# Retention in a 5-block transformer kernel: tokens on partitions for values and outputs

## The reference

```python
q, k, v, g = jnp.split(h @ w_in, [hk, 2 * hk, 2 * hk + hv], axis=-1)   # 4 heads: q, k 256 wide, v, g 512 wide
q = rotary(q); k = rotary(k) * (RET_KEY_DIM ** -0.5)                   # 256 ** -0.5 = 0.0625
o_fwd = retention_scan(q, k, v, log_gamma[0], True)                    # decay gamma ** (i - j), j <= i
o_bwd = flip(retention_scan(flip(q), flip(k), flip(v), log_gamma[1], False))
o = o_fwd + o_bwd
mu = jnp.mean(o, axis=-1, keepdims=True)
var = jnp.mean(jnp.square(o - mu), axis=-1, keepdims=True)             # per token and head, over 512 channels
o = ((o - mu) * lax.rsqrt(var + EPS)) * gn_g
return (jax.nn.silu(g) * o) @ w_out
```

## Time and profile before

| | |
|---|---|
| time, median of 3 runs | 3336.67 us (3329.39 to 3336.78) |
| profiled execution | 3337.88 us, of which the span of instructions 3335.9 us |
| PE busy | 3210.7 us, 96% |
| DVE, POOL, ACT busy | 1979.4, 1575.2, 1135.4 us |
| weight matmuls | 12096 (4032 tiles of three) |
| mean granted TensorE clock | 0.985 of full speed |

### The profile page before, as it was taken

One profiled execution on the slowest core, in us unless ns is written; L12 is line 12 of the kernel. 1 busy time (PEld: TensorE's weight loads), 2 busy tenths in 40 slices (PEclk: granted clock), 3 DMA queues, 4 the chain that ended last, 5 costly groups with the idle time before them and its releaser, 6 DMA issues. The chain is left out here.

```text
span 3335.9 us, 35062 instructions
## 1 busy us (share of the span) xinstructions
PE 3210.7 (96%) x13881; PEld 2471.9 (74%) x13881; DVE 1979.4 (59%) x2907; ACT 1135.4 (34%) x1686; POOL 1575.2 (47%) x764
## 2 busy tenths in 40 slices
PE   8889999998999999999999998898999999899999
PEld 5657888865778877777878776676778876587887
DVE  5464111288776584449477723423686588877756
ACT  5453222345422235543222322322322235542222
POOL 3224544566454453335554523433454556645454
PEclk9999999999999999999999999999999999999999
DMA  4212333321232333223332312222232332123232
GB/s 176 67 45 76 101 95 97 93 70 51 78 102 87 97 99 108 86 67 91 99 101 86 116 51 64 70 63 70 70 101 89 95 95 71 49 82 101 89 95 89
DMA packets 80675, 286.03 MB, mean 86 GB/s; under 512 B 9088, under 2 KB 9344, under 8 KB 80384
## 3 DMA queue, kind: packets, MB, share of 16 engines
q1 hardware_dynamic: 80512, 283.80, 27.2%
HBM read 281.40 MB, written 2.10 MB: 85 GB/s over the span
## 5 line engine op out<-in xcount | busy, mean ns | idle before, releaser
L2149 POOL TENSOR_TENSOR WL<-RAW,WH 128x1024 fp32r<-128x1024 f32 x504 | 1243.4, 2470 | 1362.1 <-ACT WH L1461 1361.6
L1243 PE MATMUL PS<-XH,WH 128*128 128x512 f32 x2768 | 1135.7, 410 | 44.2 <-POOL WL L2149 38.8
L1245 PE MATMUL PS<-XH,WL 128*128 128x512 f32 x2768 | 1088.0, 393 | 0.0
L1244 PE MATMUL PS<-XL,WH 128*128 128x512 f32 x2768 | 1087.8, 393 | 0.0
L1243 PEld LDWEIGHTS PS<-XH,WH 128*128 128x128 f32 x2768 | 525.5, 190 | 221.1 <-issue 89.7
L1461 ACT ACTIVATE WH<-RAW 128x1024 fp32r<-128x1024 f32 x504 | 526.5, 1049 | 430.6 <-PE PS L1245 430.0
L1244 PEld LDWEIGHTS PS<-XL,WH 128*128 128x128 f32 x2768 | 526.1, 190 | 114.6 <-issue 14.2
L1245 PEld LDWEIGHTS PS<-XH,WL 128*128 128x128 f32 x2768 | 525.0, 190 | 114.0
L1243 PE MATMUL PS<-HH,WH 128*128 128x512 f32 x1264 | 500.9, 396 | 15.4 <-DVE HL L2046 9.6
L1244 PE MATMUL PS<-HL,WH 128*128 128x512 f32 x1264 | 494.4, 391 | 0.0
L1245 PE MATMUL PS<-HH,WL 128*128 128x512 f32 x1264 | 494.3, 391 | 0.0
(11 more groups left out here) (225 smaller groups left out, 2359.3 us busy)
## 6 DMA issues: line engine op xcount, KB each, us to landing
RAW<-wst SPq DMA_DIRECT2D x504, 512.0 KB, 3.5
BI<-natb SPq DMA_DIRECT2D x16, 384.0 KB, 4.6
X<-xin SPq DMA_DIRECT2D x16, 256.0 KB, 5.0
X<-cmpw SPq DMA_DIRECT2D x1, 2048.0 KB, 9.5
out<-X SPq DMA_DIRECT2D x8, 256.0 KB, 2.1
BI<-relm SPq DMA_DIRECT2D x4, 448.0 KB, 10.0
PRM<-prm SPq DMA_DIRECT2D x1, 685.0 KB, 12.4
BI<-rope SPq DMA_DIRECT2D x2, 256.0 KB, 4.0
```

The lines of the kernel that those rows point to most:

```text
L1243: e.matmul(o, wh, h, start=first, stop=False)
L1244: e.matmul(o, wh, l, start=False, stop=False)
L1245: t = e.matmul(o, wl, h, start=False, stop=last)
L2149: e.tensor_tensor(WL[:, b % NSPLIT, :], RAW[:, b % NRAW, :], WH[:, b % NSPLIT, :].bitcast(f32), SUB).then_inc(*did(lo_made, ("lo", b)))
```

## The change

What it does, all inside the retention layer and the layout of its weights:

- Weights of v are laid out so that a block holds one input chunk's 512 output columns of the head. `by_tokens` takes four tiles at once and issues `mac_tokens` four times, once per group of 128 tokens, into four banks: the tokens' slice is stationary, the 512 weight columns move. ACT evacuates each bank with the per-token factor as a per-partition scale (`to_values`). `to_tokens` is gone from this layer.
- `rs_tokens` turns the per-token factor once by four transposes to get it on partitions (G8 columns 4 to 7). `rope_scale` multiplies cos and sin by the factor once, and `rotate_1` and `rotate_2` multiply straight from the PSUM bank, so q and k need no `scaled`. The factor 0.0625 moves into the product of `ret_scores`.
- The scores are deferred steps due 8, 11, 14 and 17 tiles into the value tiles, the values come as deferred beats among the gates' tiles (6, 10, 14, 18, 22).
- `ret_values` has PT stationary and the values moving: the bank holds 128 tokens by 512 channels. `bn_stats` and `bn_aggr` read mean and variance from it along the free axis, ACT makes the reciprocal root of one column, and `ret_centre` evacuates with both as per-partition scalars. `ret_mean`, `ret_var`, `ret_sum` and their matmuls are gone.
- `ret_out` transposes back by 128 x 128, four per chunk, and one DVE operation multiplies bank, gain and gate. Silu of all four gates is one deferred step after the gates.

```diff
+def spans(name, mc):
+    if name.startswith("ret_in"):
+        return (0, 4, False), (4, 8, True), (8, mc, False)
+    return (0, wide(name), True), (wide(name), mc, False)
...
+            def by_tokens(mv, evac):
+                group = [banks.get() for _ in range(4)]
+                for k, (h, l, made) in enumerate(mv):
+                    four = [take_tile() for _ in range(4)]
+                    b, j = four[0][0:2]
+                    ends = k == len(mv) - 1
+                    for t, bank in enumerate(group):
+                        done = ("tokens", state["tile"], t)
...
+                        step("mac_tokens", bank.ap, (*(bank.free if k == 0 else ()), made), k == 0, ends, b, j, t, h, l,
+                             events)
+                        flush_ready()
+                        if ends:
+                            evac(t, bank, done)
...
-                    linear(norm["mv"], 12, evac, mid=(lambda: norm_stats(norm)) if h == 0 else None, pace=1)
-                    flush()
...
+                    linear(norm["mv"], 4, rotate, mid=start if h == 0 else None, pace=1)
                     for j in range(4):
...
+                        later(scores(j), 8 + 3 * j)
+                    by_tokens(norm["mv"], to_values)
+                    for u in range(5):
+                        later(beat(u), 6 + 4 * u)
+                    linear(norm["mv"], 4, gate, pace=1)
+                    later(silus, 0 if h == 3 else 2)
                     for c in range(4):
...
+                        later(finish(c), (64 if h == 2 else 0) + 4 + 2 * c)
+                    return cur
...
+            def mac_tokens(i, o, after, first, last, b, j, t, h, l, events):
+                wh, wl = (x[:, b % NSPLIT, 128 * j:128 * j + 512] for x in (WH, WL))
+                hs, ls = (x[:, 128 * t:128 * t + 128] for x in (h, l))
...
+                e.matmul(o, hs, wh, start=first, stop=False)
+                e.matmul(o, ls, wh, start=False, stop=False)
+                t = e.matmul(o, hs, wl, start=False, stop=last)
...
-                    t = e.matmul(bank, v[:, 128 * j:128 * j + 128], PT[:, pt, j, :], start=j == 0, stop=j == 3)
+                    t = e.matmul(bank, PT[:, pt, j, 128 * u:128 * u + 128], v[j], start=j == 0, stop=j == 3)
...
+            def rotate_2(i, bank, x2, a, x1, c, free, made, i0):
...
+                e.tensor_tensor(a, bank, sinv, MUL).then_inc(*did(dve_made, (i, "a")))
+                e.tensor_tensor(x2, bank, cosv, MUL).then_inc(*did(dve_made, (i, "x2c")))
+                w.wait_ge(*at((i, "a")))
                 e.tensor_tensor(x1, x1, a, SUB).then_inc(*did(dve_made, (i, "x1")))
...
+                e.bn_stats(s6, bank).then_inc(*did(dve_made, (i, "six")))
+                w.wait_ge(*at((i, "six")))
+                e.bn_aggr(mv, s6).then_inc(*did(dve_made, (i, "stats")))
...
+                e.tensor_scalar(o, bank, mean, rs, SUB, MUL).then_inc(*did(dve_made, (i, "o")))
```

More of the change, by code:

```diff
@@ L1126, in ret_layer, with start, turn @@
                 dm_free = [bias_free]
+                rt = G8[:, 4:8]
+                def start():
+                    norm_stats(norm)
+                    st["rope"] = step("rope_scale", norm["rs"].ap, norm["rs_made"])
+                    def turn():
+                        bank = banks.get()
+                        i = step("rs_tokens", norm["rs"].ap, norm["rs_made"], rt, bank.ap, bank.free)
+                        bank.done((i, "rt"))
+                        norm["z"] = (i, "tr")
+                        st["rt"] = (i, "rt")
+                    later(turn, 8)
                 def head(h):
-                    qk, vts, gs = {}, [], []
+                    qk, vts, gs, cur = {}, [], [], {}
+                    pt = h % 2
                     def decay():
@@ L1166, in head @@
[L1166 to L1170, removed]
-                    for c in range(4):
[L1172 to L1210, removed]
@@ new lines, in scores, with f @@
+                    def scores(j):
+                        def f():
+                            bank = banks.get()
+                            i = step("ret_scores", j, [qk[n][0].ap for n in range(4)], (qk[1][1], qk[3][1]), bank.ap,
+                                     bank.free, pt, (st["dm"], *pt_free[pt]))
+                            bank.done((i, "p"))
+                            if j == 3:
+                                cur["p"] = (i, "p")
+                                dm_free[0] = (cur["p"],)
+                                for n in range(4):
+                                    qk[n][0].done((i, "mm"))
+                        return f
@@ L1419, in ret_scores, with rs_tokens, ret_values @@
                     *did(pe_made, (i, "mm")))
-            def ret_values(i, v, made, pt, bank, bank_free, o, o_free):
+            def rs_tokens(i, rs, rs_made, rt, bank, bank_free):
+                for event in bank_free:
+                    w.wait_ge(*at(event))
+                w.wait_ge(*at(rs_made))
+                turn4(rs, bank, 4, (i, "tr"))
+            def ret_values(i, u, v, made, pt, bank, bank_free, s6, mv, rs):
                 for event in (*bank_free, *made):
@@ L1431, in ret_mean @@
                 w.wait_ge(*at(made))
[L1432 to L1437, removed]
-                e.matmul(bank, ones, s0, start=True, stop=True).then_inc(*did(pe_made, (i, "mm")))
+                for u in range(4):
+                    t = e.transpose(bank[:, 128 * u:128 * u + 128], os[u][:, 128 * c:128 * c + 128], ident)
+                t.then_inc(*did(pe_made, (i, "tr")))
             walk(dict(
-                mac=mac, rsqrt=rsqrt, to_tokens=to_tokens, pair_scores=pair_scores, pair_turn=pair_turn,
+                mac=mac, mac_tokens=mac_tokens, rs_tokens=rs_tokens, rsqrt=rsqrt, to_tokens=to_tokens, pair_scores=pair_scores, pair_turn=pair_turn,
                 pair_values=pair_values, lru_gates=lru_gates,
```

211 lines of the change are left out of this document (114 added, 97 removed).

## The result

The changed kernel takes 3273.95 us (median of 4 runs, 3271.2 to 3275.65) against 3334.88 of the kernel before in the same comparison (median of 4, 3329.39 to 3336.78): the ratio is 0.9819, interval 0.9802 to 0.9836, or 60.9 us less. 3280 was forecast. The profiled execution took 3271.2 us, span 3269.4.

A forecast was written before the change was run, and what follows sets the result against it. PE, busy 96%, was taken as the bound: the retention stretch falls from 507.2 to 449 us (work 439.2, waits 6, 1 and 3), -58 from the profiled 3337.9, giving 3280 us; range 3270 to 3292, chance 0.70.

The forecast's parts named there:

- 61.6 us that are no work, 20 of them the clock: Retention layer's 507.2 us: PE work 445.6, the other 61.6 being 41.5 of PE waits and 20 mostly matmuls at 1.2 GHz.
- PE work -6.9 + 0.45: PE in the layer: eight mean and variance matmuls go (-6.9 us), the transposes of `rs_tokens` come (+0.45), leaving 439.2.
- rival 3: Token matmuls with weights moving run like an f32 record, 0.43: 78 us more, 3358 us; chance 0.05.
- The wait of 18.5 is the rotation's: Ahead of the values' transposes: `scaled` queues on DVE behind the keys' rotation and stops PE; all 18.5 us go.
- The waits for WL come from mean and variance: Low half of a weight block: ACT and DVE waiting on each other delays its split; 15.4 us of PE waits go.
- rival 1: Weight stream stays late, `ret_out`, HH and HL falling into the next head's first blocks: 22 us more, 3302; chance 0.13.
- Spreading takes the 3.5 us for the last score tile: Scores and values placed between weight matmuls: PE's 3.5 us wait for the last score tile goes, switching costs nothing.
- Rotation against POOL's split, 1.2 to 1.9 per head: Before scores 0, a two-SBUF-input operation of `rotate_2` meets POOL's split: PE waits 1.5 per head, 6 us, no slow clock.
- HL at the last head, 4.1 us: Fifth HL wanted 12.7 us after the gates' end, its chain takes 8.9: the 4.1 us wait goes.
- 1 us at the layer's start, and 3 for what I did not see: Allowances for PE waits in the layer: 1 us at its start as now, 3 us for the unseen.
- rival 2: The waits move: 28 more f32 groups wait 1.5 us each for their producers, 42 us, 3322; chance 0.05.
- rival 4: Fewer than 7 spare tiles force the beats out early into a block; half of the 61.6 us stays, 3311; chance 0.04.

The follow-up runs named there:

- run 1: The changed kernel with the four score steps due four tiles later (12, 15, 18, 21); 3268.10 us, ratio 0.9801 to the kernel before.
- run 7: The changed kernel with the two products of `rotate_2` written into PSUM banks, score due times unchanged; 3267.33 us, ratio 0.9801 to the kernel before.
- Run 4: The changed kernel with the rotation undone: q and k evacuated by `scaled`, rotated by six operations in SBUF; 3297.33 us, ratio 0.9889 to the kernel before.
- run 5: The changed kernel with eight f32 matmuls more, two per head, into banks the next transposes overwrite; 3282.06 us, ratio 0.9846 to the kernel before.
- run 3: The kernel before with one part of the change alone, q and k rotated straight from the bank; 3302.60 us, ratio 0.9905 to the kernel before.
- run 6: The kernel before with the transposes of the value chunks deferred by 12 tiles in place of 3; 3307.43 us, ratio 0.9923.
- run 10: run 3 with the variance due at 10 tiles, `ret_out`, HH and HL due chunk by chunk, forcing only below 4 spare tiles; 3292.58 us, ratio 0.9876.
- run 2: The changed kernel with scores, value products and centring in one block behind the gates' tiles, not spread; 3271.64 us, ratio 0.9813 to the kernel before.
- the second expectation: Text written ahead of a retry of run 8: run 3 with the variance step due 17 tiles after a head, forced only below 4 spare tiles; 3303.03 us.
- run 8: run 3 with the step of variance, `ret_out`, HH and HL due 18 tiles after a head, not 14 (74, not 72, at head 2); 3303.25 us, ratio 0.9901.

## Why the prediction was right

The layer was to fall by 58 us and fell by 59.4; the whole, by the medians, by 60.9.

- *61.6 us that are no work, 20 of them the clock.* Held, but for 1.9. With all waits gone (runs 1 and 7) the stretch is 441.1; PE's work was put at 439.2, so by the same measure 59.7 of the 61.6 could go, 41.5 of waits and 18.2 behind them. In the trace of before, 14.6 of the 18.2 are weight matmuls that start more than 0.227 apart behind the eight waits of 3.4 us and more. Granted clock 1.00 with the waits gone. Run 4 brought the low clock back behind waits of 4.9 to 5.2 us; four waits of 1.5 (the changed kernel) did not. That these would be harmless was right, but the reason given, that 2.56 us of waiting had left the clock alone, does not carry: see the last section.
- *PE work -6.9 + 0.45.* The 6.9 held (run 5: 6.9 for eight). No run tries the 0.45 by itself.
- *Weights as the moving side at 0.227.* Held in the trace of after; rival 3 is out.
- *The wait of 18.5 is the rotation's.* Held: run 3 takes 16.2 of it by shortening DVE's queue, run 6 takes 14.6 by distance. They are two cures for the same thing, so their 31.3 and 25.0 us must not be added.
- *The waits for WL come from mean and variance.* The 15.4 us went, as forecast, but the cause given was in the main wrong. 6.2 of it went with the rotation (run 3), by the timelines through the decay table's exponential on ACT. Of the other 9.2, 7.3 went when `ret_out`, HH and HL were cut up by chunks (run 10), with all the operations of mean and variance kept. The changed kernel has no wait for WL, so rival 1, which feared just these HL in the first blocks, did not come. It has a `ret_out` of one operation of 749 ns with an input in PSUM, HL of 1.30 us on average where they were 1.71, and four steps two tiles apart. Which of these it needs is not shown: no run gives the changed kernel its burst back.
- *Spreading takes the 3.5 us for the last score tile.* It did, and brought 5.9. The second was forecast (1.5 per head, 6 us), and with it the sum of the two is a loss; run 2 puts that loss at 3.3 us.
- *Rotation against POOL's split, 1.2 to 1.9 per head.* The 1.5 taken held, in part by luck. Both cases came: POOL first in the first head, 1.52 where 1.9 was worked out, and the subtraction first in the other three, 1.46 where 1.2 was. The split was put at 2.6 us and took 2.39 in the one case and 2.9 in the other. Run 7 shows the cause, since only where the products lie was changed. The rule of the Trainium skill (SBUF — State Buffer, "SBUF: two separate sides"), that a VectorE operation with two SBUF inputs is locked out for the whole of a GpSimd operation that reads SBUF and came first, agrees: 2.86 us, ending 0.55 behind POOL. So does POOL's side: 2.93 in place of 2.39 in the heads where the subtraction goes through, though by the records POOL starts 0.01 us ahead of it there. (The prediction counts six to eight operations of the old rotation as reading twice from SBUF. It is six: the two products with 0.0625 have one tensor input and took 0.42 us each.)
- *HL at the last head, 4.1 us.* Gone. The chain was shorter than put down: its first HL ends at 2284.35, about 6.7 us behind the last gate group where 8.9 was worked out, since the first `ret_out` starts before the last silu.
- *1 us at the layer's start, and 3 for what I did not see.* The 1 is in no view: PE is idle 0.1 us there. Together the two were 2.7 (447.8 less 439.2 and 5.9): 0.8 the restarts behind the four waits, and the 1.9 that are left in runs 1 and 7. The forecast of the whole was 6 us high: 1.4 of it in the layer, 3.0 because it started from the profiled execution's 3337.9 and that comparison's median of before is 3334.9, and 1.6 is within the spread of runs.
- *The range, 3270 to 3292.* Its ends do not follow from its sentence. 3270 less 2 is 3268, where runs 1 and 7 are, and 3292 does not take in rival 1 at 3302.

Rivals 2 and 4 are out by the waits of PE, and rival 1 as said. Forcing by too few tiles exists, though: it is how the second expectation explains run 8, in the layer as it was before.

From run 3 to the changed kernel the stretch falls by another 28.1 us. 6.5 of it are PE's work, 13.2 waits (19.1 to 5.9), and the rest, 8.4, what stood behind the long waits.

Not tried: tokens on partitions with the statistics still on PE. What the layout by itself is worth, apart from making bn_stats possible, is only in the counts (16 groups of transposes out, 17 in).

The versions of runs 1 and 7 come out below the changed kernel: 3268.1 and 3267.3 us, 6 to 7 less by the medians, with 6.7 us less of stretch in each trace. The intervals of the ratios overlap, but the highest execution of either (3270.31 and 3268.13) is below the lowest of the changed kernel (3271.2).

## What to carry to other kernels

Where PE is busy 96% of the time, list what it waits for in the stretch, and add the matmuls at the lower clock behind the long waits: here 41.5 us of waits cost some 60. Several short waits are cheaper than one long one of the same sum: run 10 took only 3.5 us of waits from run 3, and 9.8 us of time. Before making work on another engine smaller, try to move its consumer: 9 tiles of distance in one place had 25 us, 4 tiles in another 6.7. Steps that all engines take in order should be short: a burst of several chunks blocks unrelated work queued behind it (the weights' split), and moving the burst whole only changes which block is late.

## What the runs showed of the hardware

- In the layer of all twelve traces, every tensor_tensor of 512 columns with an input in PSUM that ran beside an operation of POOL took 0.67 to 0.70 us, and writing to PSUM made it hardly slower (products written to a bank: 700 ns). With both inputs in SBUF it lasted up to 2.9 us.
- POOL's operations are longer too where DVE reads twice from SBUF. HL took 1.71 us on average before, where `ret_out` has both inputs in SBUF, and 1.30 in the changed kernel, where it has one in PSUM. In the same layers the split of a block took 2.53 and 2.46 on average, and 2.41 in run 7.
- One input in SBUF is not always safe. In run 8 the tensor_scalar of the decay table, whose only tensor input is in SBUF, took 2.76 us and ended 0.48 us behind POOL's operation; in the kernel before, where it never met POOL, it took 0.68. Those 0.68 us are for 896 columns, as much as a tensor_tensor takes for 512. (Timelines of DVE and POOL.)

```profile
1994.72 2.76 DVE L2087 TENSOR_SCALAR BI<-BI,SM 128x896 f32<-128x896 f32 x1
...
1994.21 2.79 POOL L2165 TENSOR_TENSOR WL<-RAW,WH 128x1024 fp32r<-128x1024 f32 x1
```

- bn_stats of 512 columns from PSUM takes 699 ns, like a plain read of them, and bn_aggr 182.
- Weights moving and activations stationary run at the same 0.227 us per matmul as the other way round.
- The length of a wait near 2.6 us does not settle the clock. In run 3 PE waited 2.65 us for a weight block at the same place of two heads. Behind the first the starts are 0.23 apart; behind the second they are 0.43 apart from the sixth matmul on. Of six such waits in three traces (2.56 to 2.65), the two before had no slow matmuls behind them, of the two in run 3 the second did, and in run 6 both did. In the layer, in these traces, no wait of 2.0 us or less started a slow stretch, and those of 3.3 and more did.

```profile
1995.89 0.47 PE L1256 MATMUL PS<-XH,WH 128*128 128x512 f32 x1 [2.65 <-POOL WL L2165]
...
1996.89 0.39 PE L1257 MATMUL PS<-XL,WH 128*128 128x512 f32 x1
1997.12 0.40 PE L1258 MATMUL PS<-XH,WL 128*128 128x512 f32 x1
```

```profile
2092.06 0.47 PE L1256 MATMUL PS<-XH,WH 128*128 128x512 f32 x1 [2.65 <-POOL WL L2165]
...
2093.30 0.63 PE L1258 MATMUL PS<-XH,WL 128*128 128x512 f32 x1
2093.73 0.63 PE L1256 MATMUL PS<-XH,WH 128*128 128x512 f32 x1
```
